# The mLSTM's four projections in seven half-size products each, with their steps reordered around them

## What is computed

```python
h = rms(x, lp['norm_mix'])
proj = h @ lp['w_in']
(lru_x, lru_g, q_lat, kv_lat, k_rp, r_q, r_k, r_v, r_g,
 m_q, m_k, m_v, m_o, m_if) = jnp.split(proj, ...)
y_d, (C_new, n_new, mm_new) = mlstm(m_q, m_k * MLSTM_DK ** -0.5, m_v, ig, lf, m_C, m_n, m_m)
y_d = head_rms(y_d.reshape(B, T, -1), on[3 * G:]) * jax.nn.sigmoid(m_o)
x = x + jnp.concatenate([y_a, y_b, y_c, y_d], axis=-1) @ lp['w_out']
```

## Time and profile before

| what | value |
|---|---|
| median of 3 runs | 928.46 us (928.31 to 929.08) |
| the profiled execution | 928.3 us |
| its span, first to last instruction | 926.5 us |
| PE busy in the span | 920.3 us (99%) |
| DVE, ACT, POOL busy | 498.6, 209.9, 444.4 us |
| granted TensorE clock | 1.0 throughout |
| TensorE's share of the chain that ended last | 98% |

### The profile page before, as it was taken

One profiled execution on the slowest core, in us unless ns is written; L12 is line 12 of the kernel. 1 busy time (PEld: TensorE's weight loads), 2 busy tenths in 40 slices (PEclk: granted clock), 3 DMA queues, 4 the chain that ended last, 5 costly groups with the idle time before them and its releaser, 6 DMA issues.

```text
span 926.5 us, 14897 instructions
## 1 busy us (share of the span) xinstructions
PE 920.3 (99%) x5712; PEld 812.7 (88%) x5712; DVE 498.6 (54%) x1018; ACT 209.9 (23%) x457; POOL 444.4 (48%) x469
## 2 busy tenths in 40 slices
PE   8999999999999999999999999999999999999998
PEld 6777877778999999999977678777799999999998
DVE  6674656845565656512363665577356556563221
ACT  3224255432000000100132244462310011100001
POOL 6210380125966666676411215403268666666670
PEclk9999999999999999999999999999999999999999
DMA  9969312129555554433434673112655555533321
GB/s 280 237 131 98 112 46 92 52 17 251 138 139 141 142 141 144 134 129 126 133 124 136 30 147 96 47 48 50 138 150 141 143 142 143 147 125 126 131 94 39
DMA packets 159636, 113.02 MB, mean 122 GB/s; under 512 B 10247, under 2 KB 157357, under 8 KB 159437
## 3 DMA queue, kind: packets, MB, share of 16 engines
q1 hardware_dynamic: 154660, 104.50, 39.0%
q0 software_dynamic: 4272, 6.80, 7.3%
q10 hardware_dynamic: 632, 0.75, 0.3%
HBM read 108.46 MB, written 2.27 MB: 120 GB/s over the span
## 4 chain that ended last, share of the span: by engine, by line
PE 98%; DMA 1%; ACT 0%; SPq 0%; DVE 0%; issue 0%; DVEq 0%; ACTq 0%
PE ps L1133 52%; PE ps L785 20%; PE ps L1090 8%; PE ps L1151 2%; PE ps L891 1%; PE ps L860 1%; PE ps L987 1%; PE ps L927 1%; PE ps L1028 1%; PE ps L1037 1%; PE ps L813 1%; PE ps L833 1%; PE ps L970 1%; DMA arena<-in_x_sample 1%; PE ps L1048 1%; PE ps L1069 0%
## 5 line engine op out<-in xcount | busy, mean ns | idle before, releaser
L785 PE MATMUL ps<-hT,ring 128*128 128x320 f32 x608 | 169.4, 434 | 0.3 <-DVEq L433 0.3
L602 POOL TENSOR_TENSOR work<-ring 128x512 f32<-128x512 f32 (+1 forms) x66 | 81.8, 1239 | 153.7 <-issue 113.4
L785 PEld LDWEIGHTS ps<-hT,ring 128*128 128x128 f32 x608 | 113.7, 190 | 45.6 <-DVEq L433 0.8
L1133 PE MATMUL ps<-mixT,ring 128*128 128x160 f32 x672 | 105.0, 299 | 0.0
L1133 PE MATMUL ps<-hT,work 128*128 128x160 f32 x672 | 98.5, 299 | 0.0
L1133 PE MATMUL ps<-hT,ring 128*128 128x160 f32 x672 | 98.1, 299 | 0.0
L1133 PEld LDWEIGHTS ps<-mixT,ring 128*128 128x128 f32 x672 | 95.8, 190 | 0.0
L1133 PEld LDWEIGHTS ps<-hT,ring 128*128 128x128 f32 x672 | 93.7, 190 | 0.3
L1133 PEld LDWEIGHTS ps<-hT,work 128*128 128x128 f32 x672 | 93.7, 190 | 0.0
L604 POOL TENSOR_TENSOR work<-ring 128x512 f32<-128x512 f32 (+1 forms) x66 | 82.4, 1248 | 5.2
L603 POOL TENSOR_TENSOR ring<-ring 128x512 f32<-128x512 f32 (+1 forms) x66 | 82.2, 1246 | 5.2
(11 more groups left out here) (398 smaller groups left out, 1389.9 us busy)
## 6 DMA issues: line engine op xcount, KB each, us to landing
ring<-in_w_gu SPq DMA_DIRECT2D x88, 512.0 KB, 5.2
ring<-in_w_in SPq DMA_DIRECT2D x44, 512.0 KB, 7.2
ring<-in_w_down SPq DMA_DIRECT2D x32, 512.0 KB, 4.4
ring<-in_w_out SPq DMA_DIRECT2D x16, 512.0 KB, 4.4
ring<-in_w_down SPq DMA_DIRECT2D x16, 384.0 KB, 3.4
cst<-in_consts POOLq DMA_DIRECT2D x1, 1664.0 KB, 12.2
ring<-in_w_in SPq DMA_DIRECT2D x2, 640.0 KB, 5.5
arena<-r POOLq DMA_DIRECT2D x8, 160.0 KB, 17.4
```

What stands on the lines that cost most here:

```text
L602: step(tt(s3, a11, a21, ALU.subtract))
L785: ins = mm(bank(use, 0, T, m), w[:, k, c:c + m], right[:, k, 0:T], start=(k == 0), stop=(k == KT - 1))
L1133: ins = mm(bank(use, at * HT, HT), left, right(k), start=(opens and k == 0 and at == 0), stop=(closes and k == n - 1), skip_group_check=True)
```

## The change

Each of the four mLSTM projections becomes a `feature_pair`: seven products of four matmuls of 160 columns, in three banks a, b, c (a two-by-two split of the weights' inputs and outputs and of the columns). POOL makes three weight sums for each (`pair_weights`, four operations), VectorE makes four half sums of h once per layer (`half_sums`) and puts each result together (`pair_result`), with ScalarE copying the first product (`pair_first`). The bank list is new. The mq, mk, mo results go to SBUF and ScalarE copies mq and mk on from there; mv is written straight to where its transposes read it. The transposes mvt0 and mvt1 are moved behind the latent queries and wait for the finished mv. The scans come right behind mv's result and ahead of the query copies. POOL's weight sums stand ahead of its output stores. The output gate's sigmoid moves ahead of the value copies on ScalarE. In layer 0 state_tables stands ahead of mo's result, and lam_tables is split: `lam_begin` stays early, the rest goes behind `queries(2)` in the attention.

```diff
@@ layer_uses
-    d("ql0", "ql1", "kvr", "mo0", "mo1", "mgt", "mv0", "mv1")
-    u += [("cnT", (4,)), ("qms", (5,))]
-    d("mvt0", "mvt1")
-    u += [("qt0", (6,)), ("qt1", (7,)), ("qt2", (2,))]
-    d("mq0", "mq1", "mk0", "mk1")
+    d("ql0", "ql1", "kvr")
+    u += [("moa", (2,)), ("mob", (6,)), ("moc", (1,)), ("mgt", (0,)), ("mva", (5,)), ("mvb", (7,)), ("mvc", (4,))]
+    u += [("cnT", (6,)), ("qms", (0,)), ("qt0", (1,)), ("qt1", (2,)), ("qt2", (6,)), ("mvt0", (5,)), ("mvt1", (7,))]
+    u += [("mqa", (4,)), ("mqb", (0,)), ("mqc", (3,)), ("mka", (1,)), ("mkb", (2,)), ("mkc", (7,))]
+    dense[0] = 0
@@ gpsimd
+            def pair_weights(l, i):
+                name = PAIRS[i]
+                w, _ = quarters(name, l)
+                s2, s3, s4 = (pair_sums[i % 2][:, s] for s in range(3))
+                if i == 0 and l == 0:
+                    wait_filled(pool, "ql1", l)
+                elif i == 1:
+                    wait_filled(pool, "kvr", l)
+                    if l == 0:
+                        pool.wait_ge(sem("rows_turned"), 3)
+                elif i > 1:
+                    wait_used(pool, PAIRS[i - 2], l)
+                wait_chunk(pool, name, l)
+                a11, a12, a21, a22 = w[:, :, 0, 0, :], w[:, :, 1, 0, :], w[:, :, 0, 1, :], w[:, :, 1, 1, :]
+                tt = nc.gpsimd.tensor_tensor
+                step(tt(s3, a11, a21, ALU.subtract))
+                step(tt(a21, a21, a22, ALU.add))
+                step(tt(s2, a21, a11, ALU.subtract))
+                step(tt(s4, a12, s2, ALU.subtract), "mixed")
...
+                for i in range(NPAIR):
+                    pair_weights(l, i)
                 need(pool, "ckv_new", l, 1)
@@ tensor
+            def feature_pair(name, l):
...
+                if i > 0:
+                    need(pe, "mixed", l, MADE, i + 1)
+                    one(a, 0, lambda k: w[:, k, 0, 0, :], half(0, 0), True)
+                    one(a, 2, lambda k: w[:, k, 1, 0, :], half(1, 0))
+                    fill(one(a, 1, lambda k: s2[:, k, :], half_sum(3)), a)
+                    claim(pe, b_, l)
+                    one(b_, 0, lambda k: w[:, k, 0, 1, :], half_sum(1), True)
+                    fill(one(b_, 1, lambda k: s3[:, k, :], half_sum(2)), b_)
+                    claim(pe, c, l)
+                    one(c, 0, lambda k: s4[:, k, :], half(1, 1), True)
+                    fill(one(c, 1, lambda k: w[:, k, 1, 1, :], half_sum(4)), c)
+                    return
...
             def value_tiles(which, l, p):
                 claim(pe, u, l)
-                need(pe, "v_raw", l, 4, (0 if which == "mv" else 2) + p + 1)
+                if which == "mv":
+                    need(pe, "pair_made", l, NPAIR, 2)
...
-                for p in range(2):
-                    value_tiles("mv", l, p)
                 for t in range(NT):
                     claim(pe, f"qt{t}", l)
...
+                for p in range(2):
+                    value_tiles("mv", l, p)
...
+                feature_pair("mq", l)
+                feature_pair("mk", l)
@@ scalar
+                def pair_first(name):
+                    i = PAIRS.index(name)
+                    if i > 0:
+                        need(act, "pair_made", l, NPAIR, i)
+                    wait_filled(act, f"{name}a", l)
+                    step(A(pair_p1, bank(f"{name}a", 0, HT), ACT.Copy), "p1_copied")
...
+                pair_first("mq")
+                need(act, "pair_made", l, NPAIR, 3)
+                for n in range(4):
+                    rs = slice(n % 2 * HD, n % 2 * HD + HD)
+                    step(A(qh[rs, n, :], raw[rs, n // 2, :], ACT.Copy), "mq_ready")
+                pair_first("mk")
+                need(act, "pair_made", l, NPAIR, 4)
                 for p in range(2):
-                    step(A(kf[:, p, 0:T], bank(f"mk{p}", 0, T), ACT.Copy, scale=0.125), "mk_ready")
+                    step(A(kf[:, p, 0:T], raw[:, 2 + p, :], ACT.Copy, scale=0.125), "mk_ready")
@@ vector
+                def half_sums():
+                    h_at = lambda j, t: hT[:, j::2, t * HT:(t + 1) * HT]
+                    step(v.tensor_tensor(hp[:, 0], h_at(0, 1), h_at(0, 0), ALU.subtract), "h_sums")
+                    step(v.tensor_tensor(hp[:, 1], h_at(1, 1), h_at(0, 1), ALU.subtract), "h_sums")
+                    step(v.tensor_tensor(hp[:, 2], h_at(1, 1), hp[:, 0], ALU.subtract), "h_sums")
+                    step(v.tensor_tensor(hp[:, 3], h_at(1, 0), hp[:, 2], ALU.subtract), "h_sums")
+                def pair_result(name):
...
+                    need(dve, "p1_copied", l, P1S, PAIRS.index(name) + 1)
+                    step(v.tensor_tensor(u2, p1, bank(a, HT, HT), ALU.add))
+                    step(v.tensor_tensor(c11, p1, bank(a, 2 * HT, HT), ALU.add), bank_read=(a, l))
+                    wait_filled(dve, b_, l)
+                    step(v.tensor_tensor(halves(u34), halves(bank(b_, 0, T)), u2..., ALU.add))
+                    step(v.tensor_tensor(c22, u34[:, HT:T], bank(b_, 0, HT), ALU.add), bank_read=(b_, l))
+                    wait_filled(dve, c, l)
+                    step(v.tensor_tensor(mid, halves(u34), halves(bank(c, 0, T)), ALU.add), ...)
...
                 query_latents(1)
+                half_sums()
                 if l == 0:
+                    lam_begin()
                     key_copies(PAST_TILES, 0)
...
-                for p in range(2):
-                    wait_filled(dve, f"mo{p}", l)
-                    step(v.tensor_scalar(gate[:, p, :], bank(f"mo{p}", 0, T), SIG_MIN, None, ALU.max), "gate_arg")
+                if l == 0:
+                    state_tables()
+                pair_result("mo")
...
                 step(v.tensor_tensor(hi(krr[:, :, :]), hi(krr[:, :, :]), hi(rt), ALU.add), "krope_new")
+                pair_result("mv")
                 need(dve, "kvr_gif_done", l, 2, 2)
                 step(v.scalar_tensor_tensor(out=lfr[:, :], ...))
+                scans()
                 need(dve, "qlat_rstd", l, 1)
...
+                pair_result("mq")
                 need(dve, "q_stats", l, 2, 2)
...
+                pair_result("mk")
                 key_copies(range(3), KTILES - 3)
```

More of the change, by code:

```diff
@@ L787, in feature, with one, half, half_sum @@
                     fill(ins, use)
+            def feature_pair(name, l):
+                i = PAIRS.index(name)
+                w, _ = quarters(name, l)
+                s2, s3, s4 = (pair_sums[i % 2][:, s] for s in range(3))
+                a, b_, c = f"{name}a", f"{name}b", f"{name}c"
+                def one(use, at, left, right, opens=False):
+                    for k in range(KT // 2):
+                        ins = mm(bank(use, at * HT, HT), left(k), right(k), start=(opens and k == 0),
+                                 stop=(k == KT // 2 - 1), skip_group_check=True)
+                    return ins
+                def half(jj, t):
+                    return lambda k: hT[:, 2 * k + jj, t * HT:(t + 1) * HT]
+                def half_sum(n):
+                    if i == 0:
+                        need(pe, "h_sums", l, 8, n)
+                    return lambda k: hp[:, n - 1, k, :]
+                wait_chunk(pe, name, l)
+                claim(pe, a, l)
+                if i > 0:
[10 more added lines that the diff above has]
+                    return
+                one(a, 0, lambda k: w[:, k, 0, 0, :], half(0, 0), True)
+                one(a, 2, lambda k: w[:, k, 1, 0, :], half(1, 0))
+                if l > 0:
+                    need(pe, "mixed", l, MADE, i + 1)
+                    claim(pe, c, l)
+                    one(c, 0, lambda k: s4[:, k, :], half(1, 1), True)
+                    claim(pe, b_, l)
+                    one(b_, 0, lambda k: w[:, k, 0, 1, :], half_sum(1), True)
+                    fill(one(b_, 1, lambda k: s3[:, k, :], half_sum(2)), b_)
+                    fill(one(a, 1, lambda k: s2[:, k, :], half_sum(3)), a)
+                    fill(one(c, 1, lambda k: w[:, k, 1, 1, :], half_sum(4)), c)
+                    return
+                claim(pe, c, l)
+                one(c, 1, lambda k: w[:, k, 1, 1, :], half_sum(4), True)
+                claim(pe, b_, l)
+                need(pe, "mixed", l, MADE, i + 1)
+                one(b_, 0, lambda k: w[:, k, 0, 1, :], half_sum(1), True)
+                fill(one(b_, 1, lambda k: s3[:, k, :], half_sum(2)), b_)
+                fill(one(a, 1, lambda k: s2[:, k, :], half_sum(3)), a)
+                fill(one(c, 0, lambda k: s4[:, k, :], half(1, 1)), c)
@@ L933, in _ @@
                     pe.wait_ge(sem("consts_loaded"), 16 * 5)
[L934 to L937, removed]
+                    pe.wait_ge(sem("ct_ready"), 1)
+                feature_pair("mq", l)
+                feature_pair("mk", l)
                 need(pe, "ckvT", l, 1)
@@ L958, in _ @@
                 key_tiles("mkt", l, "mk_ready", 2)
-                need(pe, "mq_ready", l, 2)
+                need(pe, "mq_ready", l, 4)
                 def d_scores(h):
@@ L1127, in product @@
```

(18 more changed lines are left out.)

88 lines of the change are left out of this document (49 added, 39 removed).

## The result

The changed kernel takes 934.57 us as the median of four runs (934.37 to 934.77), the kernel before 928.39: a ratio of 1.0066, 95% interval [1.0053, 1.0078]. It is slower by 6.2 us. The profiled execution took 934.64 us, its span 932.8 (before 926.5), with a mean granted clock of 0.998.

What follows compares the result with a forecast made beforehand. TensorE, busy 99% of the span, was taken as the bound. Waits of 13.0 us, less 0.3 of old wait and 8.1 of TensorE's work, gave +4.6: 932.9 us, own range 930.5 to 935.5, over all cases 920.0 to 937.5.

Steps and rivals of the forecast that it cites:

- TensorE's work, -8.1: Eight projections on TensorE, each from 8.61 to 7.60 us, 1.01 less: -8.1 us in all.
- Contention decides: Both layers: while POOL's weight sums run, VectorE gets one operation with two SBUF inputs through per sum, about 1.35 us.
- Small operations are held in full: Rotary-key operations of 48 to 96 columns beside POOL sums: held like 160-column ones, 1.3 us each.
- The upper price: Small held VectorE operations cost 1.31 us each, total +4.6; the lower reading, 0.21 to 0.26 us, gave -3.1.
- Half sums to 30.3, lam_begin 0.5: Layer 0, VectorE: half sums end at 30.3 us, then lam_begin takes 0.5 us; ckv_new comes at 45.1.
- Layer 0: 4.1 us at mvt0: Layer 0: TensorE finishes the latent queries at 54.3, mv's result ends at 58.3, so it waits 4.1 us before mvt0.
- the list of signs: Expected profile: shorter projections, 3 to 4 us waits at value transposes, rotary rows at 1.3, waits at mgt and ds0.
- Layer 1: 7.4 us: Layer 1 waits of TensorE: 0.9 at kvr's bank, 1.5 at mgt's, 3.1 for mv's result, 1.9 at mkt and ds0.
- The chain to glb, 1.9 us a layer: After mv's result: 26.7 us chain on VectorE and ScalarE against TensorE's 24.8; late 0.7 at mkt, 1.2 at ds0.
- The clock, rival (d): Slow clock stretch after each of two long waits (4.1 and 3.1 us), 1.9 us each, 937 or so; chance 0.12.
- Waits in all were put at 13.4: Sum of TensorE's new waits in both layers: 4.1 + 1.9 + 7.4 = 13.4 us, taken as 13.0 after 0.4 off.

Runs made afterwards that it cites:

- e1: Changed kernel with only 8 of every 128 columns of the weight sums made, products taking plain quarters instead (projections not computed): 919.73 us.
- e4: Changed kernel with only POOL's timing altered: mk's weight sums wait for the rotary key's block, layer 1's mo sums for normalise: 930.78 us.
- e5: Changed kernel with every weight sum made in two halves of 256 columns instead of one of 512, no step moved: 928.42 us.
- e9: Changed kernel with only lam_begin's two small operations moved ahead of the half sums in layer 0: 933.47 us.
- e6: Changed kernel with ScalarE's key norms moved from ahead of rT's and gx's copies to behind the key transposes' copy: 932.81 us.
- e3: Changed kernel with seven idle products put into layer 0's two waits, two ahead of ckv_new and five ahead of qms: 933.70 us.
- e7: Changed kernel with rotary key ahead of mq's result, lam_begin ahead of half sums, key norms behind glb, POOL's mo, mv, mq sums retimed: 924.86 us.
- e8: The kernel of e7 with the weight sums split into halves of 256 columns: 921.95 us.
- e10: The kernel of e8 with every weight sum in four pieces of 128 columns: 929.63 us.
- e11: The kernel of e8 unchanged, timed against the kernel before the change: 921.56 us, median of five runs, ratio 0.9921.

## Why the prediction was right, and where its steps were not

- *TensorE's work, -8.1.* Right: 7.61 us a projection against 7.60, and e1 gives the whole of it.
- *Contention decides.* Right, and shown: e1 takes nearly all of the sums away, e4 moves them, e5 shortens them, and the time follows each.
- *Small operations are held in full.* The upper price was right (1.1 to 1.3 us, even 4 columns), for the reason given: what is added is what was left of POOL's operation. The row behind it was read a little too evenly: of the 22 units in the earlier trace rows 20 took 1.31 to 1.32 us, two 0.32.
- *Half sums to 30.3, lam_begin 0.5.* Too low. The half sums ended at 32.35: VectorE began 0.5 us later in this execution while POOL's first sum did not, the first half sum was slow ahead of any sum (1.22 us), and two were held. lam_begin took 2.5. I had written that lam_begin costs 0.5 in the same paragraph that had the sums running; the rule was not applied to my own list. ckv_new came at 48.6 instead of 45.1. e9 shows that this term is not worth its face value, though: move it and the next operation is held.
- *Layer 0: 4.1 us at mvt0.* The place was wrong. The waits stand earlier, 0.6 at cnT and 1.8 at qms, for the banks of mo's middle product and of mgt, which mo's result and the gate rows free late. The term behind it is ckv_new, 3.5 us later than I had it: with 45.1 mgt's bank would have been read at about 49.6, and qms wanted it at about 49.8 (an estimate from the prediction's own times). e5, where ckv_new came at 45.0, has the picture I drew: no wait at cnT and qms, 2.3 us at mvt0. I followed POOL's queue and VectorE's list in layer 0, but no bank of PE between mo and mvt0, so the list of signs had no place for this. The rotary block began at 53.8, so only two of its seven were held, not four.
- *Layer 1: 7.4 us.* Measured 6.2, at the places named: 0.9, 1.2, 2.6, 0.4 and 1.1 against 0.9, 1.5, 3.1 and 1.9. The holds are those counted as well: 2.0 us on normalise, three half sums of 1.8, three small operations.
- *The chain to glb, 1.9 us a layer.* Measured 0.36 + 1.12 = 1.5. e6 confirms its last link. That it is late for its own length is wrong: in e1, where hardly anything is held, there is no wait at all.
- *The clock, rival (d).* It happened, behind waits of 0.6 and 1.8 us and not the 4 us that I had thought of. It added 1.8 us to the latent queries, but was nearly free, since PE would have waited next (e3).
- *Not in the sum:* about 0.2 us for each wait beyond its listed length, some 2 us over nine waits. Back to back, a matmul's start lies some 0.17 us before the end of the record ahead of it; behind a wait that overlap is missing as well.

Waits in all were put at 13.4 and were 10.0. The slow stretch (1.8), the 0.2 per wait and 0.8 of start-up and middle made up for what was missing. So the mechanism was right, layer 0's places were not, and that the sum came as near as it did (+4.6 against +6.2) is in part luck: terms that offset each other.

## What to carry to other kernels

Before work is added to POOL, list VectorE's operations with two SBUF inputs that will run in the same microseconds, and charge each with what is left of POOL's operation beside its own length: a small one pays as much as a large one. Where they can't be kept apart in time, cut POOL's operations, as long as its own queue does not become the bound: here halves of 0.73 us gained 6.2 us with nothing moved, and quarters, at 8.6 us of sums for 7.6 us of products, lost it again. Moving one held operation away helps little while sums go on, since the next one is held in its place.

## What the runs showed of the hardware beyond that

- Scans are held as operations with two SBUF inputs are: 1.46 us beside a sum against 0.68 alone (e7).
- A clamp of 640 columns with one SBUF input, 0.49 us alone, took 0.67 in layer 0 of the changed kernel and 0.86 in e8 beside sums, by the same measure: 0.33 and 0.51 us were left of the sum. Behind it in e7, where it came first with 0.49, a sum took 1.56 instead of 1.27. The Trainium skill, SBUF — State Buffer, section Who interferes with whom, says that such instructions contend when they run in their two-port mode; no run here shows in which mode it ran.
- Ahead of any sum, while POOL issues DMAs (26 us, layer 0), the first such operation of VectorE was slow in some kernels: 1.22 us against 0.83 in the changed one, 0.82 and 1.05 against 0.17 in e9 and e7, but 0.16 in e10. No run tests what it is held by.
- The fall of the clock is not a matter of a wait's length alone. After 0.58 and 1.83 us it fell; in e4 after 0.76 and 1.65 at the same place it stayed at 1.00; behind the wait of 2.65 in layer 1 it stayed in the changed kernel and in e9, and fell in e3 and e6. What the runs share is that each fall inside the two layers came during a wait of 1.4 to 4.4 us or up to 2 us behind it, and that before, e1, e8 and e11, with no wait over 0.6 us there, have no fall. The Trainium skill, TensorE: Matmul & The Clock Gate, section Part 1: The HAM clock gate, calls the number of slow matmuls at a kernel's start run-variable. The executions agree for the middle of one: the same changed kernel had mean clocks from 0.995 to 0.998. What decides in each case stays open here.
